# A streaming encoder layer on one core: the input GEMM as 7 block products in place of 8

## The reference, cut to what matters

```python
u = rmsnorm(x, norm_g) @ W_in          # x: 1152 tokens x 2048, W_in: 2048 x 7688
# A: chunk-band attention, 8 heads of 64     B: mLSTM, 4 heads of 128
# C: gated short convolution, 512 wide       D: S5 complex diagonal scan, then a GLU
x = x + concat(silu(z_g) * mixer_g(u_g)) @ W_out
y = rmsnorm(x, final_g)
```

## Time and profile before

| | before |
|---|---|
| median of 3 runs | 2232.6 us (2231.74 to 2233.89) |
| span of the profiled execution | 2230.6 us |
| TensorE busy | 2210.9 us, 99% |
| VectorE busy | 837.7 us, 38% |
| ScalarE busy | 490.9 us, 22% |
| GpSimd busy | 413.3 us, 19% |
| DMA | 304.36 MB, mean 136 GB/s |

### The profile page before, as it was taken

How to read it: one execution, slowest core, us unless ns; L and a number is a source line. 1 busy time by engine, 2 the same in 40 slices (tenths; PEclk the granted TensorE clock), 3 DMA queues, 4 the chain that set the end, 5 groups by cost and what they waited for, 6 DMA issues and landing times.

```text
span 2230.6 us, 34685 instructions
## 1 busy us (share of the span) xinstructions
PE 2210.9 (99%) x14090; PEld 2058.1 (92%) x14090; DVE 837.7 (38%) x1446; ACT 490.9 (22%) x835; POOL 413.3 (19%) x249
## 2 busy tenths in 40 slices
PE   8999999999999999999999999999999999999998
PEld 6999999999999999999999999999998998888887
DVE  7940131313222111138657332332421463353634
ACT  6510222222221111110111111111101023333432
POOL 0122221212222122223122222212221210000000
PEclk9999999999999999999999999999999999999999
DMA  9422314142242433342322224443334556564552
GB/s 372 133 80 99 142 62 166 54 156 90 77 151 81 165 110 125 139 129 87 102 90 78 73 74 144 132 134 113 109 108 169 205 195 240 170 246 159 200 205 94
DMA packets 166862, 304.36 MB, mean 136 GB/s; under 512 B 28508, under 2 KB 105948, under 8 KB 164208
## 3 DMA queue, kind: packets, MB, share of 16 engines
q1 hardware_dynamic: 158704, 286.77, 37.8%
q10 hardware_dynamic: 8064, 16.25, 2.2%
HBM read 244.88 MB, written 76.92 MB: 144 GB/s over the span
## 4 chain that ended last, share of the span: by engine, by line
PE 94%; DVE 3%; DMA 2%; ACT 0%; SPq 0%; issue 0%; POOLq 0%; DVEq 0%; ACTq 0%
PE G L950 21%; PE G L952 21%; PE G L951 21%; PE G L1333 3%; PE X L1333 3%; PE G L1334 3%; PE X L1335 3%; PE X L1334 3%; PE G L1335 3%; PE X L1088 1%; PE X L1310 1%; PE X L1048 1%; PE X L1079 1%; DMA cv<-u_scratch 1%; DVE cv L475 1%; PE X L1202 1%
## 5 line engine op out<-in xcount | busy, mean ns | idle before, releaser
L950 PE MATMUL G<-hhi,whi 128*128 128x384 f32 x2832 | 963.9, 340 | 0.0
L952 PE MATMUL G<-hhi,wlo 128*128 128x384 f32 x2832 | 948.4, 335 | 0.0
L951 PE MATMUL G<-hlo,whi 128*128 128x384 f32 x2832 | 948.0, 335 | 0.0
L950 PEld LDWEIGHTS G<-hhi,whi 128*128 128x128 f32 x2832 | 532.2, 188 | 21.1 <-issue 13.4
L951 PEld LDWEIGHTS G<-hlo,whi 128*128 128x128 f32 x2832 | 532.4, 188 | 0.8
L952 PEld LDWEIGHTS G<-hhi,wlo 128*128 128x128 f32 x2832 | 532.0, 188 | 0.0
L924 POOL CAST whi<-wr 128x1024 fp32r<-128x1024 f32 x115 | 124.4, 1082 | 1383.8 <-PE G L952 1168.1
L926 POOL TENSOR_TENSOR wlo<-wr,whi 128x1024 fp32r<-128x1024 f32 x115 | 283.8, 2468 | 9.2
L1350 ACT ACTIVATE ev<-G 128x384 f32<-128x384 f32 x162 | 79.3, 489 | 720.9 <-PE G L952 720.8
L2182 DVE TENSOR_TENSOR olo<-orw,ohi 128x1024 fp32r<-128x1024 f32 x96 | 112.1, 1219 | 155.1 <-ACT ohi L1604 154.6
L1604 ACT ACTIVATE ohi<-orw 128x1024 fp32r<-128x1024 f32 x96 | 95.3, 1050 | 165.6 <-PE X L1335 61.5
(11 more groups left out here) (392 smaller groups left out, 1994.4 us busy)
## 6 DMA issues: line engine op xcount, KB each, us to landing
wr<-w_in_t SPq DMA_DIRECT2D x118, 512.0 KB, 5.4
orw<-w_out_t SPq DMA_DIRECT2D x96, 512.0 KB, 5.3
u_scratch<-ev SPq DMA_DIRECT2D x174, 192.0 KB, 1.9
x_lo<-x_t SPq DMA_DIRECT2D x7, 1536.0 KB, 12.5
xin<-x_all SPq DMA_DIRECT2D x9, 1024.0 KB, 12.9
yr<-y_scratch SPq DMA_DIRECT2D x12, 768.0 KB, 7.7
xo<-x_all SPq DMA_DIRECT2D x3, 3072.0 KB, 11.7
kc<-k_cache SPq DMA_DIRECT2D x8, 1024.0 KB, 5.5
```

Source lines behind the costliest of these rows:

```text
L950: mm(G[:, j, 0:GC], whi[:, kh, k], hhi[:, kk, hs], start=(kk == 0), stop=False)
L951: mm(G[:, j, 0:GC], whi[:, kh, k], hlo[:, kk, hs], start=False, stop=False)
L952: return mm(G[:, j, 0:GC], wlo[:, kh, k], hhi[:, kk, hs], start=False, stop=(kk == 15))
```

## The change

The GEMM of a pair of tiles by two quarters of the tokens (QN = 288) is a 2 x 2 product of blocks: two halves of the inner rows, two tiles, two token quarters. A scheme of Strassen's kind (Winograd's form) makes it with 7 block products in place of 8. A block product is a `piece`: 24 matmuls of 288 columns. The tokens are two halves, one after the other, with 30 pairs of tiles in each: 2 x 30 x 7 = 420 pieces, HALF = 210.

- **Operands of the tokens.** 7 blocks of 128 x 2304 (4 quarters of the input and 3 or 4 sums of them), each with high and low part, are made at the start for quarters 0 and 1, and again at HALF for quarters 2 and 3, in the same place.
- **First half.** It runs alone, with nothing of the mixers between. For each pair SP loads four weight blocks `W`, VectorE makes the four sums `T` (`make_T`), SP stores them to `t_scratch`, ACT rounds the seven blocks, GpSimd subtracts all seven (`low`), ACT copies three banks out of PSUM and VectorE adds four times (`out`).
- **Second half.** It stands between the mixers' steps, as `fill(k)`: k pieces. SP loads seven weight blocks a pair (`load_O`), ACT copies seven banks, GpSimd subtracts seven blocks and makes the four additions (`add`, on 128 x 288). Within the attention GpSimd does the rounding too (POOL_CASTS, pieces 242 to 297); elsewhere ACT does it.
- **Where the pieces stand.** START 32, attention 56, streams 24, S5 45, mLSTM chunks 26, heads 8, before the GLU 2, GLU 4, convolution 13; in all 210.
- ACT's evacuation with a function is a copy and, for tiles that need it, a second pass (`apply`) on `ev`.

```diff
-            def product(kk, j):
-                kh, k = kk // 8, kk % 8
-                hs = slice(GC * j, GC * j + GC)
-                mm(G[:, j, 0:GC], whi[:, kh, k], hhi[:, kk, hs], start=(kk == 0), stop=False)
-                mm(G[:, j, 0:GC], whi[:, kh, k], hlo[:, kk, hs], start=False, stop=False)
-                return mm(G[:, j, 0:GC], wlo[:, kh, k], hhi[:, kk, hs], start=False, stop=(kk == 15))
...
+                bank = G[:, (0, 1, 0, 2, 0, 2, 1)[i], 0:QN]
+                for k in range(KH):
+                    hi = whi[n % 3][:, k]
+                    mm(bank, hi, AH[i][:, k], start=(i in (0, 1, 3, 5) and k == 0), stop=False, skip_group_check=True)
+                    mm(bank, hi, AL[i][:, k], start=False, stop=False, skip_group_check=True)
+                    last = mm(bank, WL[i][:, k], AH[i][:, k], start=False, stop=(k == KH - 1), skip_group_check=True)
+                last.then_inc(prod_done, 1)
+
+            turns = iter(range(HALF, ALL))
+
+            def fill(k):
+                for _ in range(k):
+                    piece(next(turns))
...
+            def low(n):
+                i = n % PIECES
+                if pool_casts(n):
+                    pool.wait_ge(prod_done, n - 2)
+                    pool.wait_ge(o_in[i], 16 * ((n - HALF) // PIECES + 1))
+                    g.tensor_copy(whi[n % 3][:, :, :], OR[i][:, :, :]).then_inc(hi_made, 1)
+                pool.wait_ge(hi_made, n + 1)
+                where, j = weights_of(n)
+                raw = OR[i][:, :, :] if n >= HALF else W[:, j] if where == "W" else T[:, j]
+                tt(WL[i][:, :, :], raw, whi[n % 3][:, :, :].bitcast(F), SUB).then_inc(lo_made, 1)
+
+            def add(n):
+                pp, i = divmod(n, PIECES)
+                if i >= 3:
+                    s, c, after = ((0, 0, 3), (1, 2, 5), (2, 2, 6), (3, 1, 7))[i - 3]
+                    pool.wait_ge(c_done, copies_before(pp) + after)
+                    tt(ev[:, s], ev[:, s], cp3[:, c], ADD).then_inc(out_done, 1)
...
-HEAD_AT, TURN_AT, GLU_AT, CONV_AT, LAST = 3, 15, 22, 28, 48
+X_LOADS = (96, 32, 32, 32)
+START = (7, 14, 4, 7)
+ATT_A, ATT_B = (1,) * 8, (0, 0, 1, 1, 1, 1, 1, 1)
+STREAM = (0, 1, 1, 1, 0)
+S5_FILL = ((6, 1, 5, 1), (3, 1, 5, 2), (3, 1, 5, 2), (3, 1, 4, 2))
+CHUNK, LAST_CHUNK, HEADS, TURN = (1, 1, 1), (1, 1), (1, 1), (1, 1)
+GLU = (0, 0, 1, 0, 0, 1, 0, 0, 1, 0, 0, 1)
+CONV = (1, 3, 6, 2, 1)
...
-S5_CUTS = ((0, 8, 10, 18, 18), (0, 4, 6, 15, 18), (0, 4, 6, 15, 18), (0, 4, 6, 15, 18))
```

More of the change, by code:

```diff
@@ L12 @@
 GC = NT // 3
+QN = NT // 4
+KH = KT // 2
+PAIRS, PIECES = 30, 7
+HALF = PAIRS * PIECES
+ALL = 2 * HALF
 BAND_KEYS = 640
@@ L503, in gemm @@
-            def gemm(T, kh, j, more=True, store=True):
-                if j == 0 and more:
-                    load_w(T + 1, kh)
-                if kh == 1 and store:
-                    store_u(T, j)
-            def stored(T):
-                for j in range(3):
-                    sp.wait_ge(u_stored[j], 16 * T + 32)
-            def gemms(base, step, steps, tiles, last=False):
-                for t, kh, j in gemm_segs(step, steps, tiles):
-                    gemm(base + t, kh, j, not (last and t == tiles - 1))
@@ new lines, in _, with fill, square_sum @@
+            turns = iter(range(HALF, ALL))
+            def fill(k):
+                for _ in range(k):
+                    piece(next(turns))
+            def square_sum(q, sq, kh, half):
+                pe.wait_ge(sq_done, 4 * q + 2 * kh + half + 1)
+                for k in range(4 * half, 4 * half + 4):
+                    last = mm(X[:, q, 0:QN], ones[:, :], sq[:, k], start=(kh == 0 and k == 0), stop=(kh == 1 and k == 7))
+                if kh == 1 and half == 1:
+                    last.then_inc(ssq_mm, 1)
@@ new lines, in gates @@
+            def gates(q):
+                bank = X[0:16, q, 0:QN]
+                first, second = ((0, gx[:, 0:KH]), (3, gx[:, KH:KT])) if q % 2 == 0 else ((1, gx[:, 0:KH]), (5, gdx[:, :]))
+                for n, (i, w) in enumerate((first, second)):
+                    for k in range(KH):
+                        mm(bank, w[:, k], AH[i][:, k], start=(n == 0 and k == 0), stop=False)
+                        last = mm(bank, w[:, k], AL[i][:, k], start=False, stop=(n == 1 and k == KH - 1))
+                last.then_inc(gate_mm, 1)
@@ new lines, in _ @@
+            pe.wait_ge(const_done, 14)
+            for q, sqs in ((0, (AR[2], AR[6])), (1, (AR[1], AR[2]))):
+                for kh in range(2):
+                    for half in range(2):
+                        square_sum(q, sqs[kh], kh, half)
+            for n in range(HALF):
+                if n == PIECES * NORM_AT:
+                    for q in range(2):
+                        pe.wait_ge(norm_chain, 5 + 5 * q)
+                        mm(X[:, q, 0:QN], ones[:, :], Rb[:, q], start=True, stop=True).then_inc(ssq_mm, 1)
+                if n == PIECES * (PAIRS - 1):
+                    pe.wait_ge(gate_w, 21)
+                    pe.wait_ge(ms_done, 4)
+                    gates(0)
+                    gates(1)
+                piece(n)
@@ new lines, in _, with fill, squares, root @@
+            turns = iter(range(HALF, ALL))
+            def fill(k):
+                for _ in range(k):
+                    turn(next(turns))
+            def squares(src, dst, arrived):
+                act.wait_ge(arrived, 16)
+                for half in range(2):
+                    ks = slice(4 * half, 4 * half + 4)
+                    fn(dst[:, ks], src[:, ks], ACT.Square).then_inc(sq_done, 1)
+            def root(q):
+                act.wait_ge(ms_done, q + 1)
+                fn(Rb[:, q % 2], Rb[:, q % 2], ACT.Sqrt).then_inc(rms_done, 1)
```

1249 lines of the change are left out of this document (671 added, 578 removed).

## The result

The changed kernel takes **2591.5 us** (2590.4 to 2592.4, three runs) against 2232.6: ratio 1.160, 95% interval 1.158 to 1.162. The profiled execution has a span of 2590.6. The direction was forecast; the size was not: 2373, with a range of 2255 to 2465.

A forecast was written before the change was run, and what follows sets the result against it. TensorE, busy 99%, was taken to bound the kernel: 152.6 us less of its work gives 2078, and terms for lost cover and the shared port bring 2371, median 2373 us; 80% range 2255 to 2465.

The forecast's parts named there:

- TensorE's sum: Whole kernel: 10080 matmuls at 0.1334 us, 152.6 us less TensorE work, giving 2078.0 us if all else stayed covered.
- a. Start: Ahead of the first output: VectorE and GpSimd have the seventh operand ready at about 92 us; +53 us.
- b. First half: The 30 pairs: port work 22.3 us beside TensorE's 22.4, 0.5 us a pair for hand-overs; +15 us.
- c. Turn and gates: Turn of the halves: operands remade, 20 us shown; gate chain later and stretched, 25; +45 us.
- d. Attention: Attention's 32 steps: 0.4 us a step, with the rounding on GpSimd too; +14 us, bounds 4 to 30.
- e. Streams: Streams: no piece in the first and last place of each; +14 us, bounds 8 to 22.
- f. S5: S5: VectorE's and GpSimd's work adds up on one port, 71 us a part; +82 us, bounds 50 to 115.
- g, h, i: mLSTM chunks +8 us; heads, turn to the GLU and its inputs +20; convolution's 100 us chain less covered, +42.
- The port loop binds the first half: Rival: order of subtractions and sums leaves holes, a pair takes 25 us, the kernel 2440; chance 0.20, with the clock case.
- The rival with the clock: Rival: 0.145 us spacing or stretches at the clock's low level after idle time, +50 to +70 us; within the port-loop rival's 0.20.

The follow-up runs named there:

- x1: Changed kernel with a second place for output block slot 3 in pairs 16 to 28 of the first half; 2566.0 us, ratio 1.148.
- x2: Changed kernel with SyncE issuing the stores of u ahead of weight-sum stores and weight loads in the first half; 2550.4 us, ratio 1.141.
- x7: Changed kernel with both first-half edits, x1's second place for slot 3 and x2's stores first; 2532.5 us, ratio 1.135.
- x10: x7 with TensorE's norm products of token quarters 2 and 3 one pair later (NORM_AT 15 in place of 14); 2525.4 us, ratio 1.130.
- x5: Changed kernel leaving out half of each GpSimd subtraction from the second half's third pair on, TensorE using rounded weights instead; 2529.9 us, ratio 1.132.
- x4: Changed kernel with the attention's weight roundings on ACT again in place of GpSimd; 2596.8 us, ratio 1.161.
- x9: Changed kernel with 8 pieces moved from the streams into the first two attention steps of each pair of heads; 2569.3 us, ratio 1.150.
- x14: x10's and x9's edits together, plus 8 more pieces moved from the streams to the attention; 2537.2 us, ratio 1.135.
- x6: Changed kernel with 8 pieces moved from the streams to S5, two more in each part; 2590.8 us, ratio 1.160.
- x8: Changed kernel with unread matmuls, 70 and 80, ahead of TensorE's two long waits in each part of S5; 2575.6 us, ratio 1.154.

## Why the prediction was wrong, step by step

- **TensorE's sum: right.** 0.1333 us a matmul measured, 0.1334 said; 2078 was the right base, and the 0.1225 us that the formula of the Trainium skill gives ("TensorE: Matmul & The Clock Gate", section "Back-to-back issue gap") was not reached; the page gives it for a matmul by itself, not for a stream that loads weights for each.
- **a. Start: right, in part by luck.** The first pair ended at 92.9 us, said 92. The norm's reciprocal took 1.95 us and the whole blocks 2.55, those beside GpSimd 4.75, near what was summed. But VectorE had the seventh operand ready at 83.9, 8 us earlier than said, and TensorE's last three pieces ran behind it: it had waited 15.3 us for VectorE's operands and 8.7 for GpSimd's low parts.
- **b. First half: the step that failed**, 101 in place of 15. The sum of port work per pair held: with a free place for slot 3 a pair takes 22.6 us, not 22.9. What was missing is the loop of one output block: made by VectorE at the pair's end, stored by SyncE behind the weight sums, landed 5.5 us after issue (1.9 before), and only then free for the second of ACT's three copies in the next pair. I named the queue only for the weight load, as an upper bound of 2 us a pair. x1, x2 and x7 show the loop and its price (49 us together), x10 the wait for the norm of quarters 2 and 3 (7 us of the median, 14 of the stage), which my sum left out. The rest, 38 us, is VectorE's work for the other half (pairs 14, 16 and 18 in x10) and small losses in the early pairs; that was read from the trace and not tried. Why a store lands so much later isn't shown either: the changed kernel moves 472.8 MB at a mean of 183 GB/s where it was 304.4 MB at 136, and no run separates the two.
- **c. Turn and gates: mis-sized**, 74 in place of 45. The first seven pieces after HALF took 60 to 62 us in every run, over twice what TensorE needs. In the whole stage TensorE waits 30.1 us for GpSimd's low parts (`WL`) and 19.4 for VectorE's operands (`AL`). No run takes this stage apart; x5 makes it 10 us shorter, all of it behind those first pieces, so the port has at least that part.
- **d. Attention: the second step that failed**, 69 in place of 14. I priced GpSimd's roundings and the port; x4 and x5 show that neither counts. TensorE is idle for 49 us there, 34 of them at the loads of k and z, once in every pair of heads. These loads land about 1 us later than before (6.3 and 8.1 us after issue, where it was 5.5 and 7.1), but a step is 11 us long now where it was 16, and the first two steps have a single piece: x9 puts 25.6 us of pieces there and the stage gets 6 us shorter, so it takes away 31 of the 69. What makes up the other 38 isn't shown.
- **e. Streams: near by luck.** 7, said 14, and under the lower bound of 8; x14 shows how much hangs on single pieces and on the clock there.
- **f. S5: right in mechanism**, 106 in place of 82. Halving GpSimd's work gives 36 us (x5), 8 pieces more cost 20 (x6), and the clock can be worth some 14 at most (lengths in x8). The term mis-sized is the port's sum: 75 to 78.5 us a part in place of 71. GpSimd is busy for 140 us in S5 where the sum had 127, most of that since an addition of 128 x 288 takes 1.12 us there and not 0.7; how the rest divides isn't shown.
- **g, h, i.** 27, 8 and 53 for 8, 20 and 42. The chunks vary by 16 us (139 to 155) between runs of unchanged code. The convolution's chain took 111 us in place of 100: the forecast had no port in this term, and in x5 the chain takes 102, so GpSimd's 13 subtractions on VectorE's port are most of it. (Before, 20 segments covered this stretch and not 24; the sum doesn't use that number.)
- **The rivals.** "The port loop binds the first half" had the place right and the mechanism wrong in the main. The rival with the clock was priced at 50 to 70: some 590 of the pieces' matmuls at the lower level, up to 0.24 us apart, add 59 us to TensorE's time in the whole kernel; how much of it lies beside other waits isn't shown.

The range ended at 2465 because nearly every bound was set by a duration of a row, and only the weight load's by the time that a buffer takes to come free again. Even all upper bounds together, 2522 (the prediction says 2530), lie below what was measured.

## What to carry to other kernels

When a change cuts the bounding engine's work, every loop that it used to hide gets shorter cover at once: list for each buffer who fills it, who drains it, which queue the drain stands in and behind what, and compare that round trip with the new period. Make this list before the sum of busy times; here the first half's sum held, and the loop cost more than all the slack that it left. Where one issuing queue serves two streams, put the transfer that frees a buffer ahead of those that wait for an engine.

Taking filling work out of a stage saves only what the waits behind it don't take back, and where the stage's own matmuls stand on its chain it can even get longer, since after a wait they can run at the lower level of the clock (x14).

## What the runs showed of the hardware

- A store of 144 KB to DRAM landed 5.5 us after its issue in the changed kernel (median), one of 192 KB after 1.9 us in the kernel before; with the stores first in the queue (x2) it was 4.6. The mean traffic was 183, 136 and 185 GB/s.
- The same matmuls of 128 columns with 32 columns of weights took 275 ns in a stretch with a mean granted clock of 0.94 and 409 ns in one with 0.74. The sixteen transposes of a part of S5 took 1.9 us at the upper level and 3.3 to 3.7 at the lower one, its 128 y products 4.1 and 5.8 to 6.0 (kernel before, changed kernel and x8).
- The pieces' matmuls of 288 columns, each with a load of weights, started 0.1333 us apart at the upper level and 0.240 at the lower one.
- One GpSimd subtraction of 128 x 1024 stood in VectorE's way until its end (2.36 us for 256 columns, 0.42 alone), but GpSimd's and VectorE's port work covered 21.1 us of pairs of 22.6 us (x1) and held TensorE up by 0.2 us at most. That is the exclusive lock of the Trainium skill ("SBUF — State Buffer", section "SBUF: two separate sides"); the rows agree with it, and the hand-overs cost almost nothing.
